# Order of work in the input projections of a two-layer hybrid decoder

## The reference

```python
h = rms_norm(x, attn_norm[l])
proj = h @ w_in[l]                       # 17 column groups
# A) gated DeltaNet, 4 heads x 64
qkv = silu(causal_depthwise_conv(concat(gq, gk, gv)))         # 4 taps
g = -exp(a_log) * softplus(ga + dt_bias);  beta = sigmoid(gb)
gcum = cumsum(g) in a chunk;  decay = exp(gcum_i - gcum_j)    # lower triangle
a = strict_lower((k*beta) @ k.T * decay);  solve (I + a) [u, w] = [v*beta, k*beta*exp(gcum)]
scan over chunks: v_new = u - w @ S;  o = q*exp(gcum) @ S + (q @ k.T * decay) @ v_new;  S = ...
o_gdn = rms_norm(o) * silu(gz)
# B) sparse attention, 8 query heads x 64, 2 key heads: compressed blocks, selected blocks, window
kc = rms_norm(gelu(windows(kcmp) @ w1) @ w2);  vc likewise    # 31 blocks
ks, kw = rope(rms_norm(.));  qn = rms_norm(q), qr = rope(qn);  three softmaxes, gated and added
# C) o_conv = cb * causal_depthwise_conv(cc * cx)             # 3 taps
x = x + concat(o_gdn, o_nsa, o_conv) @ w_out[l]
h2 = rms_norm(x, ffn_norm[l]);  gate, up = split(h2 @ w_gate_up[l])
x = x + (silu(gate) * up) @ w_down[l]
```

## Time and profile before

| | us |
|---|---|
| median of three runs | 1528.72 |
| the profiled execution | 1532.56 |
| its span | 1530.8 |
| TensorE matmul busy in the span | 1443.5 |
| VectorE busy | 646.9 |
| GpSimd busy | 644.6 |
| ScalarE busy | 506.9 |

### The profile page before, as it was taken

The page is one execution under the profiler, slowest core; times in us unless marked ns, Lnnn a source line. Parts: engine busy times, 40 slices in busy tenths (PEclk is TensorE's granted clock), DMA queues, the critical chain, the costliest instruction groups (busy, mean ns, idle before and its releaser), DMA issues.

```text
span 1530.8 us, 20341 instructions
## 1 busy us (share of the span) xinstructions
PE 1443.5 (94%) x8498; PEld 1213.9 (79%) x8498; DVE 646.9 (42%) x1040; ACT 506.9 (33%) x860; POOL 644.6 (42%) x369
## 2 busy tenths in 40 slices
PE   5999989989999999999988989899899999999999
PEld 4887877668988888888868878777698888888887
DVE  6527455662343402433164184565523443034421
ACT  5443223552423212231235432144524322123220
POOL 4375331553344443444423843324533434344442
PEclk9999997999999999999989999989999999999999
DMA  6214210002433223333222251200023332333322
GB/s 172 86 57 83 75 40 17 1 1 57 89 97 96 95 85 110 91 103 99 81 65 77 62 125 29 55 1 2 1 71 89 90 110 76 103 101 92 104 83 76
DMA packets 182859, 112.68 MB, mean 74 GB/s; under 512 B 46576, under 2 KB 170480, under 8 KB 182768
## 3 DMA queue, kind: packets, MB, share of 16 engines
q1 hardware_dynamic: 182768, 111.39, 26.0%
HBM read 108.49 MB, written 2.88 MB: 73 GB/s over the span
## 4 chain that ended last, share of the span: by engine, by line
PE 78%; DVE 11%; issue 4%; POOL 3%; ACT 3%; DMA 1%; SPq 1%; DVEq 0%; ACTq 0%; POOLq 0%
PE ps L543 61%; PE ps L804 2%; PE ps L652 2%; PE ps L843 2%; DVE arena L1572 2%; PE ps L900 2%; PE ps L826 1%; DVE st L258 1%; POOL arena L1401 1%; PE ps L766 1%; DVE arena L1580 1%; DVE arena L269 1%; POOL w_lo L1305 1%; DVE arena L1496 1%; PE ps L852 1%
## 5 line engine op out<-in xcount | busy, mean ns | idle before, releaser
L1305 POOL TENSOR_TENSOR w_lo<-w_raw,w_hi 128x2048 fp32r<-128x2048 f32 (+1 forms) x100 | 452.9, 4529 | 635.0 <-ACT w_hi L1032 635.0
L1032 ACT ACTIVATE w_hi<-w_raw 128x2048 fp32r<-128x2048 f32 (+1 forms) x100 | 188.6, 1886 | 560.5 <-PE ps L543 553.3
L543 PE MATMUL ps<-hT_hi,w_lo 128*128 128x512 f32 x928 | 234.0, 394 | 0.0
L543 PE MATMUL ps<-hT_hi,w_hi 128*128 128x512 f32 x912 | 228.7, 392 | 0.5 <-DVE hT_lo L1449 0.5
L543 PE MATMUL ps<-hT_lo,w_hi 128*128 128x512 f32 x912 | 226.9, 390 | 0.0
L543 PEld LDWEIGHTS ps<-hT_hi,w_lo 128*128 128x128 f32 x928 | 176.3, 191 | 36.5
L543 PEld LDWEIGHTS ps<-hT_lo,w_hi 128*128 128x128 f32 x912 | 170.6, 188 | 35.6 <-issue 0.3
L543 PEld LDWEIGHTS ps<-hT_hi,w_hi 128*128 128x128 f32 x912 | 169.3, 188 | 36.2 <-DVE hT_lo L1449 1.4
L1810 DVE TENSOR_TENSOR aT_lo<-ffn_tmp,aT_hi 128x512 fp32r<-128x512 f32 x44 | 142.1, 3229 | 30.7 <-ACT aT_hi L1047 30.7
L1876 DVE TENSOR_TENSOR ffn_tmp<-ps,ffn_tmp 128x512 f32<-128x512 f32 x44 | 30.4, 691 | 243.7 <-ACT ffn_tmp L1283 243.7
L1047 ACT ACTIVATE arena<-ps 128x512 f32<-128x512 f32 (+4 forms) x146 | 72.7, 512 | 178.2 <-PE ps L652 83.3
(11 more groups left out here) (291 smaller groups left out, 1745.5 us busy)
## 6 DMA issues: line engine op xcount, KB each, us to landing
w_raw<-in_w_gate_up SPq DMA_DIRECT2D x88, 512.0 KB, 5.1
w_raw<-in_w_in SPq DMA_DIRECT2D x20, 1024.0 KB, 5.4
w_raw<-in_w_down SPq DMA_DIRECT2D x16, 1024.0 KB, 5.1
w_raw<-in_w_out SPq DMA_DIRECT2D x32, 256.0 KB, 4.3
w_raw<-in_w_down SPq DMA_DIRECT2D x8, 768.0 KB, 4.5
w_raw<-in_w_in SPq DMA_DIRECT2D x2, 1120.0 KB, 5.6
w_raw<-in_w_in SPq DMA_DIRECT2D x2, 1056.0 KB, 6.1
x_tok<-in_x SPq DMA_DIRECT2D x4, 512.0 KB, 5.2
```

The lines of the kernel that those rows point to most:

```text
L543: mm = nc.tensor.matmul(out_ap, a(ab, k), b(bb, k), start=first and i == 0, stop=last and i == len(kts) - 1)
L1032: nc.scalar.activation(whi[:, c % 2, 0:kt * w], raw[:, c % 2, 0:kt * w], ACT.Copy).then_inc(S["w_hi"], 1)
L1305: nc.gpsimd.tensor_tensor(wlo[:, c % 2, 0:kt * w], raw[:, c % 2, 0:kt * w], whi[:, c % 2, 0:kt * w].bitcast(F32), ALU.subtract).then_inc(S ...
```

## The change

No arithmetic is added or removed, except that two VectorE instructions read an operand from PSUM where they read the copy. Steps move:

- TensorE: `gdn_cumsum` from the middle of n = 10 to n = 11; `gdn_back(4)` and `(5)` from n = 12 to n = 17; `cmp_second` from n = 21 to 22 and `cmp_third` from 23 to 24, into bank 3 instead of 7. Hop 0 no longer waits for `kcT`; hop 6 does.
- ScalarE: it makes the triangle rows instead of GpSimd; the Tanh of z moves from n = 9 to n = 12; the evictions of `gdn_back` go ahead of the three Exp; one `unroped` moves into the loop.
- GpSimd: `split_lo(5)` moves ahead of qd, the z gate behind `one_minus(1)`, `one_minus(2)` ahead of `split_lo(11)`; qd lies in the space of TD, so the zeroing waits for `gdn_back(5)`.
- VectorE: `gate_sums` to n = 11, `cmp_norm` to 22, `cmp_keys` to 24, `k_norm` to 23 and 24, `q_norm` to n = 30 to 33, and `short_conv(1)` to n = 32, behind `conv_gate(32)`.

```diff
...
         x2 = at(0, 2, 2, XW)
-        qd = at(6144, NT, GW)
+        qd = at(11264, NT, GW)
...
                 pe.wait_ge(*S.at("params", 16 * (N_PARAMS - 6), l))
+                pe.wait_ge(*S.at("gT", 6, l))
...
                 pe.wait_ge(*S.at("cmp_kn", 1, l))
-                nc.tensor.transpose(ps[:, 7, 0:NC], kcn[0:NC, 0, :], ident[0:NC, 0:NC]).then_inc(S["cmp"], 1)
+                nc.tensor.transpose(ps[:, 3, 0:NC], kcn[0:NC, 0, :], ident[0:NC, 0:NC]).then_inc(S["cmp"], 1)
...
                 if i == 4:
-                    pe.wait_ge(*S.at("scan", 1, l))
+                    pe.wait_ge(*S.at("dabs", NT, l))
                 if i == 5:
-                    pe.wait_ge(*S.at("gT", 1, l))
+                    pe.wait_ge(*S.at("A", NT, l))
...
                 pe.wait_ge(*S.at("trig", t + 1, l))
-                pe.wait_ge(*S.at("gT", 6, l))
+                if t == 0:
+                    pe.wait_ge(*S.at("gT", 4, l))
+                    pe.wait_ge(*S.at("scan", 1, l))
...
                         pe.wait_ge(*S.at("Lmask", 1, l))
-                        pe.wait_ge(*S.at("kcT", 1, l))
...
                     pe.wait_ge(*S.at("hop_act", 4 * t + 3, l))
+                    if t == 0:
+                        pe.wait_ge(*S.at("kcT", 1, l))
...
                         gdn_back(i, 3 + i)
-                        if i == 1:
-                            gdn_cumsum()
-                if n == 12:
+                if n == 11:
+                    gdn_cumsum()
+                if n == 17:
...
                     cmp_first()
-                if n == 21:
+                if n == 22:
                     cmp_second()
-                if n == 23:
+                if n == 24:
...
                 i.then_inc(S["ev_act"], 1)
...
+            def make_trig(t):
...
+                if t >= 2:
+                    act.wait_ge(*S.at("gr", t - 1, l))
+                for h in range(GH):
+                    ins = nc.scalar.activation(trig[:, t % 2, h * P:(h + 1) * P], tri[:], ACT.Copy,
+                                               scale=gsc[:, 0, t * GH + h:t * GH + h + 1])
+                ins.then_inc(S["trig"], 1)
...
                                          ACT.Tanh, scale=0.5)
-                    act.wait_ge(*S.at("gtr", 6, l))
-                    nc.scalar.activation(zt, z, ACT.Tanh, scale=0.5).then_inc(S["zth"], 1)
...
                 if n == 10:
+                    for i in range(4):
+                        act.wait_ge(*S.at("gback", i + 1, l))
+                        ev((qT, qT, kT, kT)[i][:, i % 2, :], ps[:, 3 + i, :]).then_inc(S["gT"], 1)
+                if n == 11:
+                    act.wait_ge(*S.at("g", 1, l))
+                    make_trig(0)
+                    make_trig(1)
...
                     nc.scalar.activation(gsc[:, 6, :], gsc[:, 7, :], ACT.Exp).then_inc(S["geg"], 1)
-                    for i in range(4):
-                        act.wait_ge(*S.at("gback", i + 1, l))
-                        ev((qT, qT, kT, kT)[i][:, i % 2, :], ps[:, 3 + i, :]).then_inc(S["gT"], 1)
                 if n == 12:
+                    act.wait_ge(*S.at("gtr", 6, l))
+                    nc.scalar.activation(zt, z, ACT.Tanh, scale=0.5).then_inc(S["zth"], 1)
+                if n == 17:
...
                     nc.scalar.activation(dA, dB, ACT.Exp, scale=-1.0).then_inc(S["dexp"], 1)
+                    if t < 2:
+                        make_trig(t + 2)
...
                     nc.scalar.activation(jq[:, t % 2, :], nq[:, t, :], ACT.Square).then_inc(S["qsq"], 1)
-                if n >= 32:
-                    unroped(n - 32)
...
-            unroped(2)
+                if n >= 31:
+                    unroped(n - 31)
...
 
-            def make_trig(t):
-                if t >= 2:
-                    pool.wait_ge(*S.at("gr", t - 1, l))
-                for h in range(GH):
-                    ins = nc.gpsimd.tensor_scalar(trig[:, t % 2, h * P:(h + 1) * P], tri[:],
-                                                  gsc[:, 0, t * GH + h:t * GH + h + 1], None, ALU.mult)
-                ins.then_inc(S["trig"], 1)
...
             pool.wait_ge(*S.at("g", 1, l))
-            make_trig(0)
-            make_trig(1)
+            split_lo(5)
...
             scaled(qd, gtm[:, :, 0:GW], 3).then_inc(S["qdec"], 1)
-            split_lo(5)
...
             scaled(vb, gtm[:, :, 2 * GW:3 * GW], 1).then_inc(S["vbs"], 1)
-            make_trig(2)
-            make_trig(3)
...
             pool.wait_ge(*S.at("gr", NT, l))
+            pool.wait_ge(*S.at("gback", 6, l))
...
             one_minus(0)
+            split_lo(10)
+            one_minus(1)
...
                                     ).then_inc(S["zgate"], 1)
-            split_lo(10)
-            one_minus(1)
+            one_minus(2)
             split_lo(11)
-            one_minus(2)
...
                     chain(V.tensor_copy(vcr[32 * b:32 * b + NC, cols], ps[0:NC, 3, cols]))
-                chain(V.tensor_tensor(kcn[0:NC, 1, :], kcn[0:NC, 0, :], kcn[0:NC, 0, :], ALU.mult))
+                chain(V.tensor_tensor(kcn[0:NC, 1, :], ps[0:NC, 7, 0:P], kcn[0:NC, 0, :], ALU.mult))
...
                     rows = slice(g * HEAD, (g + 1) * HEAD)
-                    ins = V.tensor_copy(kcT[rows, g, 0:NC], ps[rows, 7, 0:NC])
+                    ins = V.tensor_copy(kcT[rows, g, 0:NC], ps[rows, 3, 0:NC])
...
                 chain(V.tensor_copy(gsc[:, 7, :], ps[:, 7, 16:32]))
-                V.tensor_tensor(gsc[:, 5, :], gsc[:, 7, :], gsc[:, 2, :], ALU.subtract).then_inc(S["gcum"], 1)
+                V.tensor_tensor(gsc[:, 5, :], ps[:, 7, 16:32], gsc[:, 2, :], ALU.subtract).then_inc(S["gcum"], 1)
...
                     cmp_hidden()
-                if n == 21:
+                if n == 22:
                     cmp_norm()
-                if n == 23:
-                    cmp_keys()
...
                     gates()
-                if n == 10:
+                if n == 11:
...
                     rsqrt(chain, st[:, 5, 0:16], st[:, 3, 0:16], st[:, 7, 0:16])
-                if n in (24, 25):
-                    k_norm(n - 24)
+                if n in (23, 24):
+                    k_norm(n - 23)
...
                     q_statistics()
-                if 31 <= n <= 33:
-                    q_norm(n - 31)
-                    if n == 33:
-                        q_norm(3)
+                if n == 31:
+                    q_norm(1)
...
                     slots += 1
-                if name == "cx":
+                if n == 24:
+                    cmp_keys()
+                if n in (30, 32):
+                    g = (n - 30) // 2
...
                     short_conv(g)
+                if n == 30:
+                    q_norm(0)
+                if n >= 32:
+                    q_norm(n - 30)
```

## The result

The changed kernel takes 1502.83 us (median of 4 runs, 1502.18 to 1503.51) against 1529.45 (4 runs, 1526.11 to 1531.7) of the kernel before on the same chip: ratio 0.9828 [0.9808, 0.9847]. That is 26.6 us where 19.6 were forecast; 1509 was predicted, 1496 to 1523 its range. Between the two profiled executions it is 29.0 (1532.56 to 1503.51, span 1501.8).

What follows compares the result with a forecast made beforehand. TensorE, busy 94% of the span, was taken as the bound, with time only in idle gaps and half clock behind them. Per layer 4.2 + 0.7 - 4.5 + 4.2 + 5.2 = 9.8, 19.6 us for two: 1509, range 1496 to 1523.

Steps and rivals of the forecast that it cites:

- A: Gate sums and triangle rows: the 4.00 us gap at the cumulative sums goes, group 18 starts 6.5 us earlier.
- B: Solve and compressor up to hop 1: GpSimd meetings and a 5.3 us hop 0 gap leave 4.2 of 6.5 us.
- C: Hop 3: `k_norm` in group 24 no longer meets the z gate, 0.7 us gained per layer.
- D: The moved z gate meets the rotation of k in group 27, making hop 12 wait: cost 4.5 us per layer.
- E: `one_minus(2)` ahead of `split_lo(11)`: the 2.46 us gap and its half clock go, 4.2 us gained per layer.
- F: The second convolution, in group 32, no longer meets `split_lo(12)` and delays hop 25: 5.2 us gained per layer.
- attention and FFN are not touched: The stages behind the projections were taken to keep their time, so nothing was counted for them.
- 1 (1496): Rival: rotation and z gate miss each other, D 0, B 2 better, 16 us per layer, 1496; chance 20%.
- 2 (1520): Rival: gaps only move, hops 0 and 1 held as now, 4.5 us per layer, 1520; chance 17%.
- 3: Rival: slower, three more VectorE meetings with GpSimd splits between A and hop 1, 1537; chance 6%.
- 4: Rival: no change, each gap made up at the next wait, within 0.3% of 1529; chance 7%.

Runs made afterwards that it cites:

- glc_first: The changed kernel with VectorE's two copies of `glc` ahead of the product that releases GpSimd's scaling: 1501.95 us.
- square_copy: The changed kernel with the compressor's square read again from its SBUF copy alone: 1505.0 us.
- zgate_wait: The changed kernel with one more GpSimd wait, so the z gate starts behind the rotation of k in group 27: 1499.83 us.
- before_conv: The kernel before with only `short_conv(1)` moved, to group 32 behind `conv_gate`: 1515.69 us.
- conv_back: The changed kernel with `short_conv(1)` back in group 31: 1520.88 us.
- om_back: The changed kernel with `one_minus(2)` behind `split_lo(11)` again: 1512.9 us.
- qkmask_late: The kernel of zgate_wait with GpSimd's mask of qk moved out of the solve, behind the z gate: 1498.47 us.
- gate_early: The changed kernel with the last `conv_gate` one place earlier in attention, directly behind `key_lo(0)`: 1504.11 us.
- all_four: zgate_wait, glc_first and qkmask_late together, plus `split_lo(7)` ahead of the zeroing of TD: 1490.85 us.

## Why the prediction was right, and the term that was mis-sized

**A held, a little short.** The 4.00 gap at L625 is gone, group 18 starts 5.6 us earlier (6.5 forecast). ScalarE's eight triangle rows took 2.47 (2.3 was taken, from the earlier trace rows). What was missed is the `glc` copies, counted with the scan at 0.6: they met GpSimd's scaling by `gsc`, and the gram waited 1.52 instead of 0.3. VectorE and GpSimd after:
```profile
85.35 2.09 DVE L1556 COPY glc<-gsc 64x8 f32<-64x8 f32 x2
```
```profile
85.51 7.49 POOL L1329 TENSOR_TENSOR arena<-arena,gsc 128x1024 f32<-128x1024 f32 x4 [1.31 <-DVE gsc L1553]
...
118.20 4.12 POOL L1372 TENSOR_TENSOR arena<-arena,offblk 128x2048 f32<-128x2048 f32 x1
...
140.20 4.59 POOL L1324 TENSOR_TENSOR w_lo<-w_raw,w_hi 128x2048 fp32r<-128x2048 f32 x1 [10.62 <-ACT w_hi L1036]
...
177.85 2.39 POOL L1383 TENSOR_TENSOR arena<-arena,gng 128x1024 f32<-128x1024 f32 x1
```
glc_first shows the cause. The table load of 1.28 stands, and group 20 waits for no `w_lo`.

**B held almost to the number, in part by luck.** VectorE after, answering to the earlier trace rows:
```profile
116.78 1.48 DVE L1580 TENSOR_TENSOR arena<-arena 128x1 f32<-128x1 f32 x1 [8.44 <-DMA arena<-diag_in]
...
118.48 3.85 DVE L1580 TENSOR_TENSOR arena<-arena 128x4 f32<-128x4 f32 x1
...
122.96 0.18 DVE L1580 TENSOR_TENSOR arena<-arena 128x16 f32<-128x16 f32 x1
...
123.38 4.30 DVE L1580 TENSOR_TENSOR arena<-arena 128x25 f32<-128x25 f32 x1
...
127.93 1.71 DVE L1580 TENSOR_TENSOR arena<-arena 128x36 f32<-128x36 f32 x1
...
136.52 0.38 DVE L1582 COPY arena<-arena 128x256 f32<-128x256 f32 x1
...
140.64 0.28 DVE L1504 TENSOR_TENSOR arena<-ps,arena 31x128 f32<-31x128 f32 x1
140.95 0.27 DVE L1505 TENSOR_REDUCE st<-arena 31x2 f32<-31x128 f32 x1
141.26 3.55 DVE L1506 TENSOR_SCALAR st<-st 31x2 f32<-31x2 f32 x1
...
177.91 2.41 DVE L1613 TENSOR_TENSOR rope_k<-arena,cossin 128x64 f32<-128x64 f32 x1
...
224.78 1.54 DVE L1588 SCALAR_TENSOR_TENSOR arena<-arena,scw 128x511 f32<-128x511 f32 x2
```
Four of the first six products of the solve wait for the end of a GpSimd instruction: the first for the rest of `split_lo(7)`, then one each for the mask, `split_lo(8)` and the mask of qk. The third and fourth run free (0.17 and 0.18), since GpSimd stood idle for 0.72 us before `split_lo(8)`, where I had counted it busy without a gap. Two errors nearly cancel here: the solve's input came 5.6 us earlier and not 7.5 (115.8 on the old clock, where 113.9 was forecast), and the solve took 20.1 us and not 21.5. Tt comes 4.5 us earlier (5.0 forecast, where the groups alone would have made it 7.5), the sixteen transfers stand at 139.15 with 7.68 as before, and the gap at hop 0 is 5.02 (5.3). The PSUM square takes 0.28 and frees next to nothing, since L1506 waits until the split's end at 144.8; square_copy has it the other way round. Hop 1 is 4.5 us earlier (4.2). C came in as 0.7.

**D** was the right meeting at the right place: L1613 stands 2.41 us under the third z-gate instruction, and hop 12 waits 2.80. zgate_wait measures 3.7, against 4.5 (the gap alone had been put at 3.4).

**E and F** remove their gaps: no wait at 201.76 and 220.71, and L1588 takes 1.54 where the earlier trace rows have 5.72. Layer 0's start-corrected positions give 4.3 and 5.3 (4.2 and 5.2).

**The mis-sized term is "attention and FFN are not touched".** It was 0 and measured 7.7 us: with it the forecast for the profile, 1513, would have been 1505, near the 1503.51 measured. Without it the median would be some 1510.5 (1502.83 plus 7.7, an estimate), which is where 1509 was forecast; as it is, 1502.83 lies in the stated range but outside the forecast's own 1504 to 1515. I had even written that a changed time of attention would refute the whole reading, and it changed. By the rows the steps all stand; what fails is the sentence that a stage with unchanged code keeps its time. I looked for half clock right behind a gap, in the projections, and never opened attention's windows, where 0.84 stood in the trace of before. Of the mechanism this is shown: the code of attention is the same, its PE counts are 270 and 269, 37.65 us go with a granted clock of 1.00 and 41.5 with 0.84. In the changed kernel none of four layers has the low stretch, in the kernel before all four. In its first ten microseconds TensorE does the same in both, 62 matmuls at the full clock, busy for 6.9 of 9.9 us; the clock differs behind them. Before:
```profile
242.36:252.30 9.94, 6.88 (x62) 5.51 (x60) 5.64 (x10) 6.90 (x19) 0.95 (x1) 1.00 0.00 0
253.00:266.00 13.00, 13.00 (x63) 10.20 (x62) 6.99 (x14) 3.97 (x14) 4.40 (x8) 0.50 0.01 2
```
and after:
```profile
232.38:242.30 9.92, 6.86 (x62) 5.48 (x60) 4.64 (x7) 6.86 (x19) 0.78 (x1) 1.00 0.00 0
243.00:256.00 13.00, 11.07 (x94) 8.74 (x92) 9.10 (x20) 6.05 (x21) 7.40 (x11) 1.00 0.01 2
```

**What stays open** is what makes it appear, and so why the change takes it away. It is not set by the order of work alone: before_conv, conv_back, om_back, qkmask_late, zgate_wait and gate_early each have it in one layer and not in the other, with the same code in both. The last gap before it doesn't decide it either (gate_early), nor does a shorter stretch of projections keep the clock up (zgate_wait's are shorter, and its layer 0 has the low stretch). Half clock shortly before attention doesn't decide it: in conv_back's layer 0 TensorE ran at 0.50 from 224.2 to 231.0, and attention from 239.75 at 1.00; in zgate_wait's layer 0 it ran at 1.00 from 153 to attention's start at 227.86, and attention has the stretch. In all ten layers that have it, it begins 9 to 11 us behind attention's start. So a rival to "the gaps of the projections reach into attention" stands untested: the fall comes from attention's own thin start (gaps of 0.45, 1.14 and 1.47 us), and what the order of the projections changes is only the moment at which that start falls. By it the 7.7 us would be luck of this order, and not a yield of the removed gaps. A single step has no one price: F undone costs 18.1, done alone it gives 12.5, and its gaps with the half clock right behind them are 10.4. The projections alone lengthen by 13.1 (F), 8.7 (A's sums) and 7.4 (E) when a step is undone.

The rivals: 1 (1496) needed D to be missed, and D was met. 2 (1520) needed hops 0 and 1 to stay. 3 needed three extra meetings, and 4 gaps that are made up; neither is in the rows. In rival 2's sum, 9.4 - 6 + 1, no row stands behind the 1.

## What to carry to other kernels

Before you sum a change that takes gaps from a busy TensorE, read the granted clock in every stage, also in those that the change doesn't touch: here 7.7 of 28.6 us lay in a part of attention whose code is the same. Compare engine instructions by where they meet, since a VectorE instruction that waits for GpSimd can hand its wait on to a later one if only it is changed (here from L1504 to L1506); what helped is to move the GpSimd instruction (zgate_wait, all_four). An experiment of a few microseconds is judged by the length of its own stage in two layers, with the clock beside it, and not by the total alone.

## What was unexpected in the hardware

- GpSimd's memset (113.54, 3.52 us) held up none of VectorE's products with two SBUF inputs, each of 0.16 to 0.24 us, while the mask and the split held them up for 3.76 and 4.29. The Trainium skill, SBUF — State Buffer, section "SBUF: two separate sides", says that the lock with two SBUF inputs stands only against a GpSimd operation that reads SBUF; the rows agree.
- Very small VectorE instructions with one SBUF input waited as well, but not all: `glc`, two copies of 64x8, took 2.09 us for 0.35, and a 31x2 scale took 3.55 for 0.16. Under the same split the square with one operand in PSUM went through in 0.28, and the reduction of the 31x128 result in SBUF (L1505) in 0.27.
- The same gap of 2.80 us was followed by a granted clock of 0.83 or of 0.67 over the next 10.19 us (after, glc_first). The low stretch in attention came and went between two layers of one execution in six kernels: four times in layer 1, at 3.9 to 5.4 us, and twice in layer 0, at 3.6 (zgate_wait) and 2.3 us (gate_early).
